# Heads of feed-forward stages without GpSimd, squares summed by TensorE between upper and lower weights, and products of constants beside waits at stage ends

## What is computed

```python
def rmsnorm(x, g, eps=NORM_EPS):
    y = xf * lax.rsqrt(jnp.mean(xf * xf, -1, keepdims=True) + eps)
    return y * g
def swiglu(x, w_gate, w_up, w_down):
    return (jax.nn.silu(x @ w_gate) * (x @ w_up)) @ w_down
hdn = swiglu(rmsnorm(x, ng[0]), w_gate, w_up, w_down)
x = x + 0.5 * rmsnorm(hdn, ng[1])
```

## Time and profile before

| what | value |
|---|---|
| median of 3 runs (lowest, highest) | 3118.11 us (3117.6, 3118.14) |
| the profiled execution's own time | 3115.16 us |
| its span, first to last instruction | 3113.3 us |
| mean granted clock of TensorE | 0.959 |
| busy: PE, DVE, ACT, POOL | 2837.9, 1305.9, 1120.9, 205.7 us |

### The profile page before, as it was taken

One profiled execution on the slowest core, in us unless ns is written; L12 is line 12 of the kernel. 1 busy time (PEld: TensorE's weight loads), 2 busy tenths in 40 slices (PEclk: granted clock), 3 DMA queues, 4 the chain that ended last, 5 costly groups with the idle time before them and its releaser, 6 DMA issues.

```text
span 3113.3 us, 44121 instructions
## 1 busy us (share of the span) xinstructions
PE 2837.9 (91%) x18428; PEld 2229.3 (72%) x18428; DVE 1305.9 (42%) x2083; ACT 1120.9 (36%) x1974; POOL 205.7 (7%) x174
## 2 busy tenths in 40 slices
PE   8989878998989999789898999999796979999997
PEld 6879656887878888578796666666595856666665
DVE  5556266546557544355463121221384542222212
ACT  5444245435447222254443222222354242222222
POOL 1000001001000222110010000000102400000000
PEclk9999899999999999899999999999897989999999
DMA  8424655535534111155243899999450035999995
GB/s 338 178 93 164 258 232 226 191 135 198 190 125 164 42 55 55 41 202 190 95 162 143 342 417 416 416 416 414 179 180 12 1 122 236 415 416 415 415 417 227
DMA packets 95540, 695.29 MB, mean 223 GB/s; under 512 B 10593, under 2 KB 10721, under 8 KB 11233
## 3 DMA queue, kind: packets, MB, share of 16 engines
q1 hardware_dynamic: 95328, 692.33, 56.1%
HBM read 691.23 MB, written 1.05 MB: 222 GB/s over the span
## 4 chain that ended last, share of the span: by engine, by line
PE 85%; DVE 7%; ACT 5%; issue 2%; POOL 0%; DMA 0%; ACTq 0%; SPq 0%; DVEq 0%
PE bank L1471 14%; PE bank L726 12%; PE bank L728 11%; PE bank L727 11%; PE bank L1531 7%; PE bank L1449 4%; PE bank L1558 4%; PE bank L1793 2%; PE bank L1801 2%; PE bank L1805 1%; PE bank L550 1%; PE bank L2309 1%; PE bank L1355 1%; PE bank L1340 1%; PE bank L1343 1%
## 5 line engine op out<-in xcount | busy, mean ns | idle before, releaser
L1471 PE MATMUL bank<-weight_ring,packed_h 128*64 128x256 f32 x2176 | 285.4, 379 | 0.0
L726 PE MATMUL bank<-source_hi_lo,weight_hi_lo 128*128 128x256 f32 x864 | 254.2, 294 | 23.7 <-DVE source_hi_lo L718 10.9
L1471 PE MATMUL bank<-more_slots,packed_h 128*64 128x256 f32 x1920 | 257.0, 379 | 1.5 <-ACT packed_h L1458 1.5
L726 PE MATMUL bank<-gate_up_hi_lo,x_hi_lo 128*128 128x512 f32 x640 | 253.9, 397 | 0.0
L728 PE MATMUL bank<-gate_up_hi_lo,x_hi_lo 128*128 128x512 f32 x640 | 249.7, 390 | 0.0
L1471 PEld LDWEIGHTS bank<-weight_ring,packed_h 128*64 128x64 f32 x2176 | 196.5, 137 | 74.0 <-issue 18.1
L727 PE MATMUL bank<-gate_up_hi_lo,x_hi_lo 128*128 128x512 f32 x640 | 249.1, 389 | 0.0
L727 PE MATMUL bank<-source_hi_lo,weight_hi_lo 128*128 128x256 f32 x864 | 248.3, 287 | 0.0
L728 PE MATMUL bank<-source_hi_lo,weight_hi_lo 128*128 128x256 f32 x864 | 248.1, 287 | 0.0
L1471 PEld LDWEIGHTS bank<-more_slots,packed_h 128*64 128x64 f32 x1920 | 174.1, 137 | 69.6 <-issue 15.4
L685 DVE TENSOR_TENSOR weight_hi_lo<-weight_ring,weight_hi_lo 128x1024 fp32r<-128x1024 f32 x138 | 168.0, 1221 | 103.9 <-ACT weight_hi_lo L679 103.9
(11 more groups left out here) (540 smaller groups left out, 5529.7 us busy)
## 6 DMA issues: line engine op xcount, KB each, us to landing
weight_ring<-weight_slots SPq DMA_DIRECT2D x437, 1024.0 KB, 7.5
more_slots<-weight_slots SPq DMA_DIRECT2D x212, 1024.0 KB, 9.1
params_sb<-small_params SPq DMA_DIRECT2D x1, 3216.5 KB, 17.7
h_sb<-weight_slots SPq DMA_DIRECT2D x3, 1024.0 KB, 5.6
y_sb<-weight_slots SPq DMA_DIRECT2D x3, 1024.0 KB, 7.7
x_sb<-x_T SPq DMA_DIRECT2D x1, 1024.0 KB, 4.8
out_T<-x_sb SPq DMA_DIRECT2D x4, 256.0 KB, 2.1
params_sb<-small_params SPq DMA_DIRECT2D x1, 73.5 KB, 4.6
```

What stands on the lines that cost most here:

```text
L726: e.matmul(out, w[0], x[0], start=start, stop=False, skip_group_check=shared)
L1471: mm = e.matmul(ps[x * CAP:(x + 1) * CAP, m * FB:(m + 1) * FB], self.hc[:, c, (2 * (p % 2) + x) * CAP:(2 * (p % 2) + x + 1) * CAP], wt[:, ...
```

## The change

- POOL does nothing in a feed-forward stage's head. The lower parts of weights (0,) are made by DVE, ahead of (1,), and the eight squares are no longer added to two.
- `squares_pe` multiplies all eight squares by the column of ones (16 products of one column) and is called inside `first_gate_up_pe`, between the upper and the lower weights.
- The products with the lower weights run half by half of the chunks, each over both halves of the tokens, where they ran over all chunks for one half of the tokens and then the other.
- ACT splits (1,) and (2,), makes the deviation, and then splits (0, 0) and (0, 1). DVE makes the lower parts of (0,) and (1,), the inverse, and then those of (2,), (0, 0) and (0, 1).
- A new function `keep_clock` multiplies constants (a tile of ones by the identity repeated to 256 columns, float32) into bank 0, a result that nothing reads. `back_pe` calls it with 2 between its two sets of transposes, in all ten stages; `first_gate_up_pe` with 3 after it has taken its banks, in all feed-forward stages but the first.

```diff
--- before.py
+++ after.py
@@ -566,6 +566,12 @@
 
 
 
+    def keep_clock(self, e, count, columns=T):
+        for _ in range(count):
+            e.matmul(self.k.bank[0][:, 0:columns], self.k.par("ones"), self.k.par("ident").unsqueeze(1).to_broadcast([P, columns // P, P]), start=True, stop=True)
+
+
+
     def norm_pe(self, e):
         self.sums_pe(e, "in", [self.k.y[:, c, :] for c in range(C)], [("x_squared", self.n, c) for c in range(C)])
 
@@ -588,6 +594,8 @@
     def back_pe(self, e):
         k, n = self.k, self.n
         for q in range(TT):
+            if q:
+                self.keep_clock(e, 2)
             for c in range(C):
                 if q == 0 and c % 2 == 0:
                     k.banks.take(e, (n, "y_T", c // 2), ("x_added", n, c + 1), of=(4 + c // 2,))
@@ -806,7 +814,7 @@
             self.k.weights.done(self.slots[b][2], self.lo_key("down", b, fc))
 
     def lo_key(self, kind, *what):
-        return "weights_lo_p" if kind == "gate_up" and what[0] == 0 else "weights_lo", self.n, kind, *what
+        return "weights_lo", self.n, kind, *what
 
     def half_done(self, j):
 
@@ -870,10 +878,12 @@
 
     def act(self, e):
         k, n = self.k, self.n
-        for split in ((1,), (0, 0), (0, 1), (2,)):
+        for split in ((1,), (2,)):
             self.split_act(e, split)
         e.wait_ge(*k.ge("x_sums", n))
         e.activation(self.in_dev[:, :], k.banks.at(n, "x_sums")[:, 0:TT], ACT.Sqrt, scale=1.0 / D, bias=k.par("eps", 0, 1)).then_inc(*k.up("x_deviation", n))
+        for split in ((0, 0), (0, 1)):
+            self.split_act(e, split)
         for b in range(FFN_BLOCKS):
             for q in range(TT):
                 if b == 0 and q == 0:
@@ -906,10 +916,12 @@
 
     def dve(self, e):
         k, n = self.k, self.n
-        for split in ((1,), (0, 0), (0, 1), (2,)):
+        for split in ((0,), (1,)):
             self.split_dve(e, split)
         e.wait_ge(*k.ge("x_deviation", n))
         e.reciprocal(self.in_inv[:, :], self.in_dev[:, :]).then_inc(*k.up("x_inverse", n))
+        for split in ((2,), (0, 0), (0, 1)):
+            self.split_dve(e, split)
         e.wait_ge(*k.ge("x_inverse", n))
         for b in range(FFN_BLOCKS):
             for q in range(TT):
@@ -930,19 +942,9 @@
 
 
     def early_pool(self, e):
-        self.begin(e)
-        self.split_gate_up_lo(e, 0)
+        pass
 
     def pool(self, e):
-        k, n = self.k, self.n
-        for s in range(3):
-            two = slice(2 * s + 2, 2 * s + 4)
-            if s == 0:
-                e.wait_ge(*k.ge("x_squared", n, 1))
-            else:
-                e.wait_ge(*k.ge("squares_added", n, s - 1))
-            e.wait_ge(*k.ge("x_squared", n, 2 * s + 3))
-            e.tensor_tensor(k.y[:, 0:2, :], k.y[:, 0:2, :], k.y[:, two, :], ALU.add).then_inc(*k.up("squares_added", n, s))
         self.back_pool(e)
 
 
@@ -971,6 +973,8 @@
 
         k, n = self.k, self.n
         ps = [self.gate_up_bank(e, 0, q) for q in range(TT)]
+        if n:
+            self.keep_clock(e, 3)
         for c in range(C):
             w = self.gu_r[:, c // 4, :, c % 4, :, :].rearrange("p h m f -> p h (m f)")
             if c % 4 == 0:
@@ -979,22 +983,24 @@
             for q in range(TT):
                 for part in range(2):
                     e.matmul(ps[q][:, :], self.x_r[:, part, c, q * P:(q + 1) * P], w[:, 0, :], start=c == 0 and part == 0, stop=False)
+        self.squares_pe(e)
+        for half in range(2):
+            for m in range(2):
+                e.wait_ge(*k.ge(*self.lo_key("gate_up", half, m)))
+            for q in range(TT):
+                for c in range(4 * half, 4 * half + 4):
+                    w = self.gu_r[:, half, :, c % 4, :, :].rearrange("p h m f -> p h (m f)")
+                    mm = e.matmul(ps[q][:, :], self.x_r[:, 0, c, q * P:(q + 1) * P], w[:, 1, :], start=False, stop=c == C - 1)
+                if half:
+                    mm.then_inc(*k.up("gate_up", n, 0, q))
+
+    def squares_pe(self, e):
+        k, n = self.k, self.n
+        ps = k.banks.take(e, (n, "x_sums"), ("x_deviation", n), of=(7,))
+        e.wait_ge(*k.ge("x_squared", n, C - 1))
         for q in range(TT):
             for c in range(C):
-                if q == 0 and c % 4 == 0:
-                    for m in range(2):
-                        e.wait_ge(*k.ge(*self.lo_key("gate_up", c // 4, m)))
-                w = self.gu_r[:, c // 4, :, c % 4, :, :].rearrange("p h m f -> p h (m f)")
-                mm = e.matmul(ps[q][:, :], self.x_r[:, 0, c, q * P:(q + 1) * P], w[:, 1, :], start=False, stop=c == C - 1)
-            mm.then_inc(*k.up("gate_up", n, 0, q))
-
-    def squares_pe(self, e):
-        k, n = self.k, self.n
-        ps = k.banks.take(e, (n, "x_sums"), ("x_deviation", n), of=(7,))
-        e.wait_ge(*k.ge("squares_added", n, 2))
-        for q in range(TT):
-            for i in range(2):
-                mm = e.matmul(ps[:, q:q + 1], k.y[:, i, q * P:(q + 1) * P], k.par("one"), start=i == 0, stop=i == 1)
+                mm = e.matmul(ps[:, q:q + 1], k.y[:, c, q * P:(q + 1) * P], k.par("one"), start=c == 0, stop=c == C - 1)
         mm.then_inc(*k.up("x_sums", n))
 
     def turn_pe(self, e, b):
@@ -1028,7 +1034,6 @@
     def pe(self, e):
         self.begin(e)
         self.first_gate_up_pe(e)
-        self.squares_pe(e)
         for b in range(FFN_BLOCKS):
             if b + 1 < FFN_BLOCKS:
                 self.gate_up_pe(e, b + 1, 0)
```

More of the change, by code:

```diff
@@ L981, in first_gate_up_pe @@
                     e.matmul(ps[q][:, :], self.x_r[:, part, c, q * P:(q + 1) * P], w[:, 0, :], start=c == 0 and part == 0, stop=False)
-        for q in range(TT):
-            for c in range(C):
-                if q == 0 and c % 4 == 0:
-                    for m in range(2):
-                        e.wait_ge(*k.ge(*self.lo_key("gate_up", c // 4, m)))
-                w = self.gu_r[:, c // 4, :, c % 4, :, :].rearrange("p h m f -> p h (m f)")
-                mm = e.matmul(ps[q][:, :], self.x_r[:, 0, c, q * P:(q + 1) * P], w[:, 1, :], start=False, stop=c == C - 1)
-            mm.then_inc(*k.up("gate_up", n, 0, q))
+        self.squares_pe(e)
[8 more added lines that the diff above has]
+                    mm.then_inc(*k.up("gate_up", n, 0, q))
     def squares_pe(self, e):
@@ L993, in squares_pe @@
         ps = k.banks.take(e, (n, "x_sums"), ("x_deviation", n), of=(7,))
-        e.wait_ge(*k.ge("squares_added", n, 2))
+        e.wait_ge(*k.ge("x_squared", n, C - 1))
         for q in range(TT):
-            for i in range(2):
-                mm = e.matmul(ps[:, q:q + 1], k.y[:, i, q * P:(q + 1) * P], k.par("one"), start=i == 0, stop=i == 1)
+            for c in range(C):
+                mm = e.matmul(ps[:, q:q + 1], k.y[:, c, q * P:(q + 1) * P], k.par("one"), start=c == 0, stop=c == C - 1)
         mm.then_inc(*k.up("x_sums", n))
```

## The result

The changed kernel took 3125.72 us in the median of 9 runs (3124.95 to 3127.68), the kernel before beside it 3117.68 us (3114.69 to 3121.87): slower by 8.0 us, ratio 1.0024, 95% interval [1.0015, 1.0032]. The forecast was 3113.8 us, 4.3 us faster, with a range up to 3117.5; the sign was wrong. The profiled execution of after took 3126.42 us with a span of 3124.6. The ratios of this document leave out one execution of e9, which took 3730.20 us at a mean granted clock of 0.739.

What follows compares the result with a forecast made beforehand. PE's chain was taken as the bound, 85% of 3113.3 us. Heads -9.15, stage 1 +2.5 and +1.7, MoE ends +0.6, constants +0.1 gave -4.3 us: 3118.11 to 3113.8, range 3109.5 to 3117.5.

Steps and rivals of the forecast that it cites:

- POOL gone, DVE at 0.47, chunk 4 at S+9.9: Stages 3, 4, 6: each x_hi_lo takes 0.47 us on DVE; chunk 4 9.9 us after S (second eight transposes' start).
- Three products of constants, 0.7 to 1.3 us, covered: Before chunk 0 in those heads: 0.7 us at full clock, 1.3 at half, hidden by the wait for chunk 4 except 0.1.
- The squares are now 16 small products, not 8: Heads, after the upper products: eight took 0.81 us, so sixteen would take 1.7 us with the first's start.
- signs of being wrong: Block 1 of stage 1 before 29.5, a wait for (2,) in other heads, or half-clock periods behind chunk 4.
- Rival D: Heads: two half-clock periods fall behind chunk 4, uncovered, costing 3.4 us per head; 3124.0 us, chance 0.04.
- Gain 3.05 per head: Stages 3, 4, 6: block 1 at S+19.05 instead of S+22.10; 9.15 us for three, bounds 2.6 and 3.3 per head.
- Weights (2,) late in the first stage, 31.1 instead of 28.62: Stage 1 head: DVE splits (2,) only after the reciprocal, PE idles 2.75 us; 2.5 us lost, bounds 2.3 and 2.7.
- The 1.7 us for the clock in this stage: Stage 1: clock may fall after PE's pause, losing 0 to 3.4 us; one period taken, 1.7 us lost.
- MoE ends, 0.6 for both: Two MoE stage ends: added constants start the second transposes 0.3 us later each; 0.6 us lost, bounds 0 and 1.2.
- The Trainium skill's floor of 25 ns: Squares: by the page's floor on starts, 16 take 0.4 us; the forecast kept the row's 0.1 us step instead.
- rival C: Squares in three heads: weight loads hide behind each other, 0.025 each, 1.3 us more gain per head; 3109.9 us, chance 0.05.
- Rival E: Heads: ACT's copies, not POOL, set the pace; no 9.15 gain, squares add 0.9 in three heads; 3125.7 us, chance 0.03.

Runs made afterwards that it cites:

- e9: Kernel before plus only the two products of constants between the transposes at every stage end: 3122.52 us, before 3118.92, ratio 1.0011.
- e3: Changed kernel without any products of constants: 3123.59 us, kernel before 3119.5, ratio 1.0013.
- e2: Changed kernel with each square multiplied by 128 columns of ones instead of one in stages 3, 4 and 6: 3121.16 us, kernel before 3119.5, ratio 1.0008.
- e1: Changed kernel with the squares summed over only two chunks, three quarters of the sum left out: 3110.69 us, kernel before 3119.5, ratio 0.9977.
- e7: Kernel before with only the lower parts of weights (0,) moved from POOL to DVE, ahead of (1,): 3118.97 us, before 3118.92, ratio 0.9995.
- e5: Changed kernel; DVE adds squares to two, summed between lower-product halves; (2,) ahead of the inverse, no constants in heads: 3111.39 us, ratio 0.9974 to kernel before.
- e6: e5 without the products of constants at the stage ends: 3109.88 us, kernel before 3118.92, ratio 0.9966.

## Why the prediction was wrong, step by step

- **POOL gone, DVE at 0.47, chunk 4 at S+9.9.** Right: 0.48, and S+9.89 in the fourth stage. In the third and sixth it was S+10.76 and S+10.77, because of the next point.
- **Three products of constants, 0.7 to 1.3 us, covered.** Mis-sized by two. A product of plain float32 in the code executes as two: six are in the trace, 1.2 us at full clock (fourth stage) and 1.65 to 1.87 with part of them at half. The wait for chunk 4 covered them in one head of three; in the others they cost 0.87 each, as e3 shows (chunk 4 at S+9.89 in all three).
- **"The squares are now 16 small products, not 8", 1.7 us.** This is the step that failed. I set the 16 products of the new code beside the 8 *executed* ones of the trace. The code before has four in `squares_pe`, and the earlier trace rows shows x8; so 16 execute as 32. They take 3.5 us, not 1.7: +1.8 in each of four heads. The same row had the figure; I did not count the products in the code against it. The count goes line by line: the transposes (8 in the code, x8) and the products of split halves (16, x16) execute once each.
- **The clock behind the squares.** Missing. I looked for pauses only. PE was busy without a gap for 3.5 us, with one column for each load of 128 columns, and the clock fell behind it; with 128 columns it did not (e2). From the first square to block 1 the changed kernel takes 8.83, 10.45 and 8.84 us in stages 3, 4 and 6 and e2 7.2 in each, so the clock costs 1.6, 3.2 and 1.6: half of the 3.4, 6.8 and 3.4 us at half clock, less a little. Half-clock periods behind chunk 4 were one of my signs of being wrong. Rival D had this place (behind chunk 4) and the price of 3.4 per head at most, but another mechanism, and I gave it 0.04.
- **Gain 3.05 per head.** Measured -1.15, -2.00 and -1.15. Constants 0.9, squares 1.8 and clock 1.6 make up, within 0.1, the 4.2 us between forecast and measurement in stages 3 and 6, squares 1.8 and clock 3.2 the 5.0 in the fourth. These are 13.4 us; the total was off by 12.3. With the squares cut to two chunks, and so without the two errors, e1 gives 3.3, 3.9 and 3.2. I also took it that a head's gain reaches the end of its stage; in e1 and e7 a half-clock period near that end takes 1.2 to 1.4 us of it back.
- **Weights (2,) late in the first stage, 31.1 instead of 28.62.** The time was right (31.0), the cost was hidden behind the squares. e1 uncovers it (a pause of 3.23). In e5, with (2,) ahead of the inverse, block 1 begins at 28.37, but a new pause of 1.49 behind it makes the stage as long as 209.24 us, 1.4 more than before. The 1.7 us for the clock in this stage came out about right by luck: as a whole it lost 3.2 us where 4.2 were forecast. The forecast had the clock fall behind the pause; it fell behind the squares without one, and behind the pause of 3.23 us in e1 it did not fall (the only half-clock period of that stage begins at 203.8). In the other heads the lower products covered it, as said.
- **MoE ends, 0.6 for both.** Direction right, size off: 1.13 each, again since two products execute as four.
- **The Trainium skill's floor of 25 ns** ("TensorE: Matmul & The Clock Gate", "Wait — 56ns, not 53.3ns?"): by it alone 32 squares would be 0.8 us, an estimate from the page's figure. The trace has 3.4 us for 31 steps, 0.11 each, and with 128 columns the same 0.11 (e2). A floor is not contradicted by a longer step, but it does not set the time here; rival C falls.
- **Rival E's 3125.7** meets the measured 3125.72 by coincidence. It had ACT set the pace, chunk 4 as late as before and no gain in the heads; chunk 4 came 3 to 4 us earlier.
- **The range.** The squares and both groups of constants were too small by the same factor, so the errors added up, and a range whose bounds all rest on one count, with nothing for the clock behind the squares, could not hold that.

## What to carry to other kernels

Before pricing products that a change adds, divide the executed count in the trace by the count in the code, line by line: each product of plain float32 runs as two here, transposes and products of split halves as one, and the term that decided was half its size. Price also what a stretch does to the clock: one-column products keep PE "busy" at 0.11 us each (the weight loads are busy 3.46 of the 3.50 us, and 128 columns take no longer), and what follows them can run at 1.2 GHz. Read a gain at the end of the stage too, not only where it arises: in e7 1.4 of 2.3 us were gone by then. Give sums over many small products to an engine with time to spare: two hidden additions on DVE (1.9 us) in place of 24 executed products, and no products of constants, made the version that beat the kernel before by 9 us (e6); which of the parts gave how much of that was not taken apart.

## What was not expected of the hardware

The granted clock fell from 2.4 to 1.2 GHz while PE was busy 3.50 of 3.50 us, behind 32 one-column products, in seven of the eight profiled heads of the changed kernel and 14 of the 17 with such products in any kernel; with 128 columns and otherwise the same instructions it fell in none of three. What sets the exceptions apart is open. Half-clock periods elsewhere move a kernel by several us from run to run (31 runs of the kernel before on one chip: 3114.79 to 3124.03 us), so gains of 3 us were told apart here by the trace and not by the time. The products of constants at the stage ends raised the mean granted clock by 0.001 (e9 against the kernel before), both groups together by 0.003 (the changed kernel against e3), and both times the kernel with them was the slower one.
